# A decoder step with 32 experts on one core: one more weight slot, other turns, and other orders ahead of the experts

## Chip, cores and metric

One core of a Trainium2 chip runs the whole kernel. The metric is the device time of one execution in microseconds, median over runs; lower is better.

## What is computed

One layer of a hybrid decoder over 288 tokens: a prompt of 256 and 8 sequences of 4 new tokens each, all in float32, model width 1024. The reference, cut to what matters:

```python
z = rmsnorm(x, norm_mix_g) @ w_in                    # 1024 -> 2048: q | k | v | u, 512 each
attn = dilated_attention(q, k, v, cache_k, cache_v)  # 8 heads of 64; windows (128,1) (512,4) (2048,16)
ssm  = s5_ssm(u, h0, ...)                            # 32 groups x 64 complex states, diagonal recurrence
g    = gelu(ssm); ssm_o = g * sigmoid(g @ w_glu + b_glu)
x    = x + concat(rmsnorm(attn), rmsnorm(ssm_o)) @ w_out
h    = rmsnorm(x, norm_ffn_g)
gates = softmax(top_4(h @ w_router + b_router))      # 4 of 32 experts
x    = x + sum_over_chosen(gate * (swiglu(h @ w1[e] + b1[e]) @ w2[e] + b2[e]))
y    = rmsnorm(x, norm_final_g)                      # outputs also: k, v and the last states
```

The recurrence has the coefficient a = exp(lambda dt), whose angle is tabulated for 128 steps, and b_bar = ((a - 1)/lambda) b. The experts' weights, 32 x 12 MiB, are most of the memory that is read.

## The kernel before

The program is written engine by engine, with semaphores between them; the order of each engine's work is the order of its code. Its stages, in time:

**Start (0 to 24 us).** SP issues the loads of x (L361: rows 0 to 255 in one transfer; L362: the 32 sample rows), constants, and eleven small parameter loads on one semaphore `prm` (L366 to L383), then w_in in four parts. ACT squares the three row tiles of x with a sum (L616) and takes the square root (L619). DVE makes the reciprocal (L827) and scales the rows, `xn` = x times the scale of its row, in three operations (L829). PE transposes `xn` for eight values of j, three tiles each (`features`, L1275), ACT and DVE bring the result out of PSUM (L623, L841). Between them PE transposes the parameters (`par`, L1283), and after j = 7 the matrix c and the state h0 (L1289).

**Projections and recurrence (24 to 120 us).** PE makes sixteen blocks of the projection (`project(n)`, L1305: 8 products of 128x128 by 288 columns, two instructions each), with the transposition of b_bar after the third (L1314). DVE makes what depends on the parameters (L867 to L903: ar, ai, fr, fi, reciprocal, four products of 256 elements, `xb`), and the last three doublings, levels 4 to 6, of the angle table (`angle_level`, L904 to L911); POOL had made levels 0 to 3 (L526 to L544). Then comes, for eight pairs of groups, a loop over DVE (L928 to L961), POOL (L556 to L595), ACT and PE (`bu`, L1327; `c_h`, L1350).

**Keys and values (101 to 200 us).** Each of the eight cached sequences has five key tiles. `key_columns(n)` (L1385) transposes one tile into PSUM bank 4 + n % 2, ACT or DVE copies it out (`key_tile`, L679), and `scores(b)` (L1402) uses the five of sequence b. The order is by hand: `keys(b)` = tiles 5b to 5b+4, then `scores(b)`. The cached keys of sequence b come in by five DMAs, once the tiles of b - 2 have been transposed (L413 to L416: two buffers, a wait on `kt_ps` in SP's queue).

**Mixer output (188 to 230 us).** DVE gathers the sample rows (L1072), ACT squares the whole of the attention output `aT` (L749), DVE multiplies it by its norm weight (L1076), sums the squares (L1077) and makes two more rows of the gated unit (`glu_rows`); PE then sums over partitions (L1565) and makes the output projection (L1573).

**Router (230 to 257 us), then experts (257 to 1214 us).** Each expert has 12 pieces of 1 MiB of weights. `slots` is a list of NSLOT places of 1 MiB in SBUF, taken from buffers that earlier stages have left; piece k of turn t lies in slot (12 t + k) % NSLOT. SP fills the slots once (`fill`, L445 to L469), each after the wait that says its buffer is free, and then refills a slot when PE has used it (`refill`, L474 to L482, the DMA at L481). An expert has as many passes as its tokens need, by 32 columns a pass, counted at run time: 51 passes for 32 experts, three for experts 0, 4, 8 and others. Only the last pass of an expert lets its slots go. One pass (`pe_pass`, L1703 to L1748) multiplies by w1 (`first_product`, L1708), adds the pass before into the result, gathers the next tokens (L1653) and, after the activation, multiplies by w2 (`second_product`, L1716). The loop over experts is a hardware loop whose body holds TURNS experts one after the other, written out:

```python
with nc.Fori(0, NEXP // TURNS, ...) as g:
    for turn in range(TURNS):
        expert(turn, g * TURNS + turn, g * (16 * TURNS * NPIECE // NSLOT))
```

TURNS x 12 must be a multiple of NSLOT: the slot of a piece is fixed in the code of the body. With NSLOT 20, TURNS is 5: six rounds of five and two experts behind. **Final norm and store (1214 to 1230 us)** end it.

Of the kernel before, what the change touches and what calls it, by code (L numbers as in the profile page):

```python
# [26 lines left out]
ALU = mybir.AluOpType  # L27
# [31 lines left out]
NSLOT = 20  # L59
TURNS = 5  # L60
# [60 lines left out]
def decoder_step(nc, I, O):  # L121

    with ExitStack() as ctx:
# [43 lines left out]
        xn = uni[:, 0:3 * D].rearrange("p (t d) -> p t d", t=3)  # L167
        e_tab = uni[:, 4608:8704].rearrange("p (r i t) -> p r i t", r=2, i=NI)
# [44 lines left out]
        slots = [flat.rearrange("p (m n) -> p m n", m=2) for flat in slots] + [late_slot]  # L213
# [10 lines left out]
        def s5_buf(n):  # L224
# [51 lines left out]
        names = """x con prm win0 win1 wglu wout late gff kload0 kload1 vload0 vload1 vload2 vload3 out ss ms  # L276
# [4 lines left out]
            gex ysv b2 etab_p etab_v gmx con_rest sc osel o_ev yfin  # L281
# [4 lines left out]
        NPRM = 11  # L286
# [73 lines left out]
        def _(sp):  # L360
            sp.dma_start(x[:, 0:2, :], I["x_prompt"][0].rearrange("(t p) d -> p t d", p=P)).then_inc(S["x"], 16)  # L361
# [10 lines left out]
            with nc.allow_non_contiguous_dma(reason="parameters of a few hundred words"):  # L372
                sp.dma_start(gmx, I["norm_mix_g"][0].rearrange("(p j) -> p j", j=J)).then_inc(S["gmx"], 16)
                small(ld[0:NI, 0:2], I["ssm_log_dt"][0].rearrange("(i g) -> i g", g=2))
                small(par[0:NI, 0:P], I["ssm_a_re"][0].rearrange("(i g) n -> i (g n)", g=2))
                small(par[0:NI, P:2 * P], I["ssm_a_im"][0].rearrange("(i g) n -> i (g n)", g=2))
# [7 lines left out]
                sp.dma_start(w_in[:, 3, :, :], wv[:, 3]).then_inc(S["win0"], 16)  # L384
# [82 lines left out]
            fill(18)  # L467
            sp.wait_ge(S["cntr"], 1)
            fill(19)  # L469
# [43 lines left out]
        def _(pool):  # L513
# [10 lines left out]
            pool.memset(top[:, :, :], 0.0)  # L524
            pool.memset(tidx[:, :, :], 0).then_inc(S["zero"], 1)
            pool.wait_ge(S["exps"], 1)  # L526
            link(pool.tensor_copy(e_tab[:, 0, :, 0:1], prm[:, PA_C, :].unsqueeze(2)))
            link(pool.tensor_copy(e_tab[:, 1, :, 0:1], prm[:, PA_S, :].unsqueeze(2)))
            for level in range(4):
                m = 1 << level  # L530
                re, im = e_tab[:, 0, :, 0:m], e_tab[:, 1, :, 0:m]
                cr = bc(e_tab[:, 0, :, m - 1:m], [P, NI, m])
                ci = bc(e_tab[:, 1, :, m - 1:m], [P, NI, m])
                t1, t2 = e_tmp[:, 0, :, 0:m], e_tmp[:, 1, :, 0:m]
                link(tt(t1, re, cr, ALU.mult))
                link(tt(t2, im, ci, ALU.mult))
                link(tt(e_tab[:, 0, :, m:2 * m], t1, t2, ALU.subtract))
                link(tt(t1, re, ci, ALU.mult))
                link(tt(t2, im, cr, ALU.mult))
                ins = tt(e_tab[:, 1, :, m:2 * m], t1, t2, ALU.add)  # L540
                if level == 3:
                    ins.then_inc(S["etab_p"], 1)
                else:
                    link(ins)  # L544
# [64 lines left out]
        def _(act):  # L609
            chain = [0]  # L610

            A = act.activation
            act.wait_ge(S["x"], 32)
            act.wait_ge(S["init"], 1)
            for t, (_, n) in enumerate(TILES):
                ins = A(xn[0:n, t, :], x[0:n, t, :], ACT.Square, accum_out=st[0:n, t:t + 1])  # L616
            ins.then_inc(S["ss"], 1)
# [7 lines left out]
            act.wait_ge(S["prm"], 16 * NPRM)  # L625
# [24 lines left out]

            for n, c in enumerate([12, 13, 14, 15] + list(range(12))):
                if n == 3:
                    act.wait_ge(S["bT_ps"], 1)
                    A(bT[:, :, :], ps[:, 0:2, :], ACT.Copy).then_inc(S["bT"], 1)
# [54 lines left out]
            for n in range(20):  # L709
                key_tile(n)  # L710
# [553 lines left out]
        def _(pe):  # L1264
# [13 lines left out]
            for j in range(4):  # L1278
                features(j)
# [512 lines left out]
```

## Time and profile before

| | us |
|---|---|
| median of 3 runs | 1234.92 (1228.98 to 1236.42) |
| the profiled execution, its own time | 1231.9 |
| its span, first to last instruction | 1230.1 |
| PE busy in the span | 1071.0 (87%) |
| DVE, ACT, POOL busy | 411.3, 219.3, 79.3 |
| HBM read | 442.46 MB |

The span is what the views below divide; 1.8 us lie around it. Times in rows are microseconds from the start of the span. "x64" is a number of instructions (a float32 product is two), and "[1.05 <-DVE uni L1009]" says that the engine had been idle for so long and what released it. PEclk 1.00 is the full granted clock of TensorE.

### The profile page before, as it was taken

The page shows a single profiled execution, that of the slowest core. Times are in us where ns is not written, and L with a number is a line of the kernel's source. Part 1 is how long each engine was busy: PE and PEld are TensorE (multiplying, and loading weights), DVE is VectorE, ACT ScalarE, POOL GpSimd, SP SyncE. Part 2 cuts the span into 40 slices and gives each one's busy share as a digit, 9 for nine tenths or more (in the row PEclk, how much of TensorE's full clock was granted, in tenths as well). Part 3 has the DMA queues.
Part 4 walks back from the last instruction along what each step waited for, and adds up shares of the span by engine and source line. Part 5 has one row for each costly group of instructions (what it writes and reads, how often), then busy time and mean ns, then how long its engine had stood idle before and what let it go on. Part 6 is the DMA issues. An engine that isn't in the chain of part 4 may idle for free.

```text
span 1230.1 us, 29852 instructions
## 1 busy us (share of the span) xinstructions
PE 1071.0 (87%) x10851; PEld 488.5 (40%) x10852; DVE 411.3 (33%) x1236; ACT 219.3 (18%) x401; POOL 79.3 (6%) x117
## 2 busy tenths in 40 slices
PE   5997889999979799989998876899889868998986
PEld 3775454444424244334433321334333323333332
DVE  4899764452222122222222211222222212222212
ACT  3213432311111111111111100011111101111102
POOL 3159500000000000000000000000000000000000
PEclk9999999999999899999999988899999988999978
DMA  8426785855999999999999999999999999999995
GB/s 238 179 86 215 256 304 217 309 207 214 419 420 421 421 384 421 421 421 395 422 420 423 421 421 420 422 385 420 422 422 393 421 421 422 390 421 421 421 419 212
DMA packets 81061, 445.49 MB, mean 362 GB/s; under 512 B 16768, under 2 KB 18112, under 8 KB 32256
## 3 DMA queue, kind: packets, MB, share of 16 engines
q1 hardware_dynamic: 81024, 445.00, 89.7%
q8 instruction: 22, 0.36, 0.1%
q14 instruction: 15, 0.12, 0.0%
HBM read 442.46 MB, written 2.51 MB: 362 GB/s over the span
## 4 chain that ended last, share of the span: by engine, by line
PE 55%; DMA 19%; SPq 16%; issue 4%; DVE 3%; ACT 2%; POOL 0%; DVEq 0%; POOLq 0%; ACTq 0%
PE ps L1708 19%; SPq L481 14%; PE ps L1716 9%; DMA ring<-in_w_moe_dram 8%; DMA low<-in_w_moe_dram 5%; DMA w_glu<-in_w_moe_dram 5%; PE ps L1653 4%; PE ps L1305 4%; PE ps L1701 3%; PE ps L1685 3%; PE ps L1573 2%; DMA ring<-in_cache_k_dram 1%; PE ps L1696 1%; PE ps L1683 1%; PE ps L1733 1%
## 5 line engine op out<-in xcount | busy, mean ns | idle before, releaser
L1708 PE MATMUL ps<-ring,uni 128*32 128x512 f32 x2032 | 249.8, 625 | 63.0 <-issue 32.4
L1708 PEld LDWEIGHTS ps<-ring,uni 128*32 128x32 f32 x2032 | 62.5, 112 | 240.6 <-issue 176.3
L1213 DVE TENSOR_SCALAR uni<-ps 128x256 f32<-128x256 f32 x51 | 21.7, 425 | 312.3 <-PE ps L1708 312.3
L1716 PE MATMUL ps<-ring,uni 128*32 128x256 f32 x1792 | 106.4, 381 | 10.5 <-DMA ring<-in_w_moe_dram 10.4
L788 ACT ACTIVATE uni<-uni 128x256 f32<-128x256 f32 x51 | 21.2, 416 | 417.8 <-DVE uni L1213 417.8
L1234 DVE COPY uni<-ps 128x256 f32<-128x256 f32 x50 | 21.2, 425 | 221.0 <-PE ps L1696 221.0
L788 ACT ACT_TABLE_LOAD x51 | 65.4, 1283 | 85.7 <-issue 85.7
L1653 PE MATMUL ps<-uni 128*32 128x256 f32 x1248 | 78.2, 383 | 0.3 <-DVE uni L1155 0.3
L1716 PEld LDWEIGHTS ps<-ring,uni 128*32 128x32 f32 x1792 | 54.3, 110 | 51.9 <-DMA ring<-in_w_moe_dram 15.3
L1305 PE MATMUL ps<-accT,ring 128*128 128x288 f32 x256 | 64.6, 411 | 0.0
L1685 PE MATMUL ps<-uni 32*128 32x256 f32 x832 | 62.3, 415 | 0.0
L1685 PEld LDWEIGHTS ps<-uni 32*128 32x128 f32 x832 | 39.1, 192 | 48.3 <-issue 46.8
L1701 PE MATMUL ps<-uni 32*32 32x512 f32 x416 | 55.4, 602 | 0.0
L1305 PEld LDWEIGHTS ps<-accT,ring 128*128 128x128 f32 x256 | 48.5, 192 | 14.5 <-issue 1.7
L1228 DVE TENSOR_TENSOR uni<-low,uni 128x96 f32 x50 | 12.9, 259 | 121.0 <-issue 112.7
L792 ACT ACTIVATE uni<-ps 128x256 f32<-128x256 f32 x51 | 19.6, 385 | 183.2 <-PE ps L1716 183.2
L790 ACT ACTIVATE uni<-ps 128x384 f32<-128x384 f32 x51 | 25.0, 491 | 145.1 <-PE ps L1738 145.1
L1653 PEld LDWEIGHTS ps<-uni 128*32 128x32 f32 x1248 | 35.4, 109 | 36.0 <-issue 17.9
L1197 DVE TENSOR_TENSOR uni<-uni 128x64 f32<-128x64 f32 x204 | 44.5, 218 | 1.4
L1222 DVE COPY uni<-ps 128x256 f32<-128x256 f32 x51 | 21.7, 425 | 65.6 <-PE ps L1733 65.6
L1708 PE MATMUL ps<-tmp,uni 128*32 128x512 f32 x320 | 39.8, 613 | 1.1 <-DMA tmp<-in_w_moe_dram 1.1
L1198 DVE TENSOR_TENSOR uni<-uni 32x32 f32<-32x32 f32 x204 | 37.0, 182 | 2.1
(383 smaller groups left out, 1231.9 us busy)
## 6 DMA issues: line engine op xcount, KB each, us to landing
ring<-in_w_moe_dram SPq DMA_DIRECT2D x232, 1024.0 KB, 24.1
tmp<-in_w_moe_dram SPq DMA_DIRECT2D x38, 1024.0 KB, 25.5
kv_rows<-in_w_moe_dram SPq DMA_DIRECT2D x19, 1024.0 KB, 23.2
w_glu<-in_w_moe_dram SPq DMA_DIRECT2D x19, 1024.0 KB, 26.5
mixer<-in_w_moe_dram SPq DMA_DIRECT2D x19, 1024.0 KB, 23.8
uni<-in_w_moe_dram SPq DMA_DIRECT2D x19, 1024.0 KB, 25.7
accT<-in_w_moe_dram SPq DMA_DIRECT2D x19, 1024.0 KB, 26.2
low<-in_w_moe_dram SPq DMA_DIRECT2D x19, 1024.0 KB, 26.6
```

Of the source, the lines that this page charges most:

```text
L481: sp.dma_start(slot(turn, k), piece(following[later - 1], k2)).then_inc(landed(turn, k), 16)
L788: A(sig, glu_b, ACT.Sigmoid, scale=ALPHA).then_inc(S["sgm"], 1)
L790: A(selT, ps[:, 5, 0:3 * P], ACT.Copy).then_inc(S["selT"], 1)
L1197: tt(selg[:, 0:2, q, :], sel[:, 0:2, :], gb[:, 0:2, :], ALU.mult)
L1198: ins = tt(selg[rows, 2, q, :], sel[rows, 2, :], gb[rows, 2, :], ALU.mult)
L1305: ins = mm(ps[:, 4 + n % 2, 0:NTOK], w_in[:, c // 4, j, P * (c % 4):P * (c % 4) + P], accT[:, j, :], start=(j == 0), stop=(j == J - 1))
L1573: ins = mm(ps[:, 4 * t + 2 * a + c, :], src[:, kb, t0:t0 + P], w_out[:, 4 * a + kb, 512 * c:512 * c + 512], start=(kb == 0), stop=(kb == 3))
L1653: ins = mm(ps[quarter(q), 6, 0:NQ], sel[:, t, :], h[:, t, NQ * q:NQ * q + NQ], start=(t == 0), stop=(t == 2), skip_group_check=True)
L1685: ins = mm(ps[:, q, NQ * t:NQ * t + NQ], selT[quarter(q), P * t:P * t + P], y[quarter(q), :], start=False, stop=True, skip_group_check=True)
L1701: mm(hidden(q), pick[quarter(q), :], b1_rows[quarter(q), :].rearrange("p (g n) -> p g n", g=2), start=True, stop=False, skip_group_check=True)
L1708: ins = mm(hidden(q), xe[:, k % 2, quarter(k // 2)], slot(turn, k)[:, :, NQ * q:NQ * q + NQ], start=False, stop=(k == 7), skip_group_check ...
L1716: ins = mm(ps[quarter(q), 7, 0:NQ], mt[:, m, quarter(k - 8)], slot(turn, k)[:, m, NQ * q:NQ * q + NQ], start=(k == 8 and m == 0), stop=(k ...
```

## The change

What it does, in parts:

1. **Ring.** 21 slots in place of 20: the first two tiles of x, 1 MiB, become slot 19, filled after `posps`; the former last slot is slot 20. TURNS is 7: four rounds of seven experts and four behind (84 = 4 x 21).
2. **Start.** x comes in three transfers; the three loads behind dt and lambda have a semaphore of their own (`par`), and the fourth part of w_in is issued right after them. ACT evaluates one square root ahead of everything, squares tile 0 and the sample rows; DVE squares tile 1 by a product and a reduction.
3. **Diagonal.** Rows are no longer scaled: DVE makes three diagonal matrices `scales` (the identity times the scale of each row, at most 128x128), and `features` is a matrix product x by `scales`, which scales and transposes at once.
4. **Order on PE.** features 0 and 1, parameters, features 2 to 7, project(0), transpositions of c and h0, project(1), project(2). ACT, not DVE, brings c and h0 out of PSUM, between its copies of projections 0 and 1.
5. **Parameters and table.** The parameter chain and `xb` go to POOL, but for the reciprocal (DVE, by a handshake `pa`). All levels 0 to 6 of the angle table are on DVE, two copies and seven levels.
6. **Key tiles.** One tile more than a sequence needs is transposed ahead of each `scores`.
7. **Mixer output.** The prompt's part of `aT` is squared and scaled early, only the 32 sample columns behind the last gather; two rows of the gated unit move ahead of the wait or of the sum.

```diff
-NSLOT = 20
-TURNS = 5
+NSLOT = 21
+TURNS = 7
+        scales = uni[:, 3 * D:3 * D + 3 * P].rearrange("p (t c) -> p t c", t=3)
-        slots = [flat.rearrange(...) for flat in slots] + [late_slot]
+        slots = [flat.rearrange(...) for flat in slots] + [x[:, 0:2, :], late_slot]
...
@ SP
-            sp.dma_start(x[:, 0:2, :], I["x_prompt"][0]...).then_inc(S["x"], 16)
+            sp.dma_start(x[:, 0, :], rows[:, 0]).then_inc(S["x0"], 16)
+            sp.dma_start(x[:, 1, :], rows[:, 1]).then_inc(S["x"], 16)
...
             fill(18)
+            sp.wait_ge(S["posps"], 1)
+            fill(19)
             sp.wait_ge(S["cntr"], 1)
-            fill(19)
+            fill(20)
...
@ POOL (in place of levels 0 to 3)
+            pool.wait_ge(S["red"], 1)
+            tt(q(16), q(PA_LR), q(PA_LR), ALU.mult)
+            link(tt(q(17), q(PA_LI), q(PA_LI), ALU.mult))
+            tt(q(16), q(16), q(17), ALU.add).then_inc(S["pa"], 1)
+            pool.wait_ge(S["exps"], 1)
...
+            pool.wait_ge(S["pa"], 2)
+            tt(q(PA_FR), q(18), q(22), ALU.mult)
+            link(tt(q(PA_FI), q(20), q(22), ALU.mult))
+            pool.wait_ge(S["prm"], 16 * NPRM)
+            tt(s3(0), v3(0), fr, ALU.mult)
...
+            ins.then_inc(S["xb"], 1)
...
@ ACT
+            A(st[:, 93:94], st[:, 94:95], ACT.Sqrt)
+            act.wait_ge(S["x0"], 16)
+            A(xn[:, 0, :], x[:, 0, :], ACT.Square, accum_out=st[:, 0:1])
             act.wait_ge(S["x"], 32)
-            for t, (_, n) in enumerate(TILES):
-                ins = A(xn[0:n, t, :], x[0:n, t, :], ACT.Square, accum_out=st[0:n, t:t + 1])
+            A(xn[0:NS, 2, :], x[0:NS, 2, :], ACT.Square, accum_out=st[0:NS, 2:3]).then_inc(S["ss"], 1)
...
             for n in range(20):
                 key_tile(n)
+            key_tile(20)
             prompt_exp(0)
-            key_tile(20)
...
+            act.wait_ge(S["aT"], 4)
+            A(sqa[:, :, 0:SEQ], aT[:, :, 0:SEQ], ACT.Square).then_inc(S["sqA"], 1)
...
@ DVE
+            dve.wait_ge(S["x"], 32)
+            link(tt(xn[:, 1, :], x[:, 1, :], x[:, 1, :], ALU.mult))
+            link(dve.tensor_reduce(st[:, 1:2], xn[:, 1, :], AX, ALU.add))
...
-                ins = ts(xn[0:n, t, :], x[0:n, t, :], st[0:n, 6 + t:7 + t], None, ALU.mult)
+                ins = ts(scales[0:n, t, 0:n], ident[0:n, 0:n], st[0:n, 6 + t:7 + t], None, ALU.mult)
...
-            link(angle_level(4))
-            link(angle_level(5))
+            dve.wait_ge(S["exps"], 1)
+            dve.tensor_copy(e_tab[:, 0, :, 0:1], prm[:, PA_C, :].unsqueeze(2))
+            link(dve.tensor_copy(e_tab[:, 1, :, 0:1], prm[:, PA_S, :].unsqueeze(2)))
+            for level in range(6):
+                link(angle_level(level))
             angle_level(6).then_inc(S["etab_v"], 1)
...
+            scaled(slice(0, SEQ))
...
+            glu_rows(2)
+            dve.wait_ge(S["sqA"], 2)
             dve.wait_ge(S["aTs"], 4)
-            tt(aT[:, :, :], aT[:, :, :], bc(gat.unsqueeze(2), [P, 4, NTOK]), ALU.mult).then_inc(S["mixa"], 1)
+            scaled(slice(SEQ, NTOK)).then_inc(S["mixa"], 1)
+            glu_rows(3)
             dve.tensor_reduce(sums[:, 0, :], sqa.rearrange("p b t -> p t b"), AX, ALU.add)
-            glu_rows(2)
-            glu_rows(3)
...
@ PE
-                    ins = tp(ps[:, 4 + j % 4, t0:t0 + n], xn[0:n, t, j::J], ident[0:n, 0:n])
+                    ins = mm(ps[:, 4 + j % 4, t0:t0 + n], x[0:n, t, j::J], scales[0:n, t, 0:n], start=True, stop=True)
...
+            project(0)
+            natural_transposes()
+            project(1)
+            project(2)
+            pe.wait_ge(S["xb"], 1)
...
-            keys(0)
+            keys(0, 6)
             scores(0)
...
-            keys(1)
+            keys(6, 11)
             scores(1)
-            keys(2)
+            keys(11, 16)
             scores(2)
...
-            keys(3)
+            keys(16, 21)
             scores(3)
...
-            keys(4)
+            keys(21, 25)
...
+            key_columns(25)
             scores(4)
```

In the loop of the last four sequences the tile 5b moves in the same way ahead of `scores(b - 1)`.

## Rows read from the trace of the kernel before

**Rows 1.** Page, part 4: shares of the chain that ended last.

```profile
PE 55%; DMA 19%; SPq 16%; issue 4%; DVE 3%; ACT 2%; POOL 0%; DVEq 0%; POOLq 0%; ACTq 0%
```

**Rows 2.** Windows: stretch, PE, PEld, DVE, ACT, POOL busy, clock, DMA share, GB/s.

```profile
255.00:290.00 35.00, 33.39 (x390) 14.01 (x394) 13.09 (x56) 6.43 (x9) 0.00 (x0) 1.00 0.18 71
...
440.00:446.00 6.00, 6.00 (x60) 1.79 (x54) 1.88 (x10) 1.67 (x2) 0.00 (x0) 1.00 0.62 221
...
561.00:568.00 7.00, 7.00 (x74) 2.25 (x70) 2.05 (x10) 1.67 (x2) 0.00 (x0) 1.00 0.78 307
...
803.00:809.00 6.00, 6.00 (x62) 1.84 (x58) 1.79 (x9) 1.67 (x2) 0.00 (x0) 1.00 0.61 227
...
926.00:931.00 5.00, 5.00 (x48) 1.46 (x48) 1.50 (x9) 0.90 (x1) 0.00 (x0) 1.00 0.75 242
...
1047.00:1053.00 6.00, 6.00 (x54) 1.78 (x58) 2.05 (x10) 1.66 (x2) 0.00 (x0) 1.00 0.70 255
1053.00:1210.00 157.00, 141.00 (x1532) 60.22 (x1524) 35.74 (x136) 20.60 (x32) 0.00 (x0) 0.93 1.01 421
```

**Rows 3.** Timeline of SP, 398 to 450 us: start, length, instruction, count.

```profile
415.79 0.39 SPq L481 DMA_DIRECT2D low<-in_w_moe_dram  x1
443.07 5.47 SPq L481 DMA_DIRECT2D ring<-in_w_moe_dram  x7
```

**Rows 4.** Chain of waits in the expert stage: start, length, piece.

```profile
273.38 7.01 PE ps L1708 x64
...
289.11 7.00 PE ps L1708 x64
```

**Rows 5.** Chain of waits, 440 to 600 us.

```profile
457.59 1.32 issue
```

**Rows 6.** Timeline, 1186 to 1231 us: the last product.

```profile
1213.67 3.66 PE L1716 MATMUL ps<-ring,uni 128*32 128x256 f32 x64
```

**Rows 7.** Timeline, 5 to 24 us: squares, table load, row scaling.

```profile
6.95 1.06 ACT L616 ACTIVATE uni<-x 128x1024 f32<-128x1024 f32 x1 [3.42 <-DMA x<-in_x_sample_dram]
...
10.20 1.28 ACT L619 ACT_TABLE_LOAD   x1
...
11.94 2.06 DVE L829 TENSOR_SCALAR uni<-x,st 128x1024 f32<-128x1024 f32 x3
```

**Rows 8.** Timeline of PE from 13 us: transpositions, first products of project(0).

```profile
14.15 3.51 PE L1275 MATMUL ps<-low,uni 128*128 128x128 f32 x12 [14.15 <-DVE uni L829]
...
23.64 1.17 PE L1305 MATMUL ps<-accT,ring 128*128 128x288 f32 x2
```

**Rows 9.** Timeline, 0 to 60 us: projections 0 to 2; angle table; pair 0.

```profile
23.64 12.38 PE L1305 MATMUL ps<-accT,ring 128*128 128x288 f32 x48
...
44.30 1.22 DVE L911 TENSOR_TENSOR uni<-tmp 128x1024 f32<-128x1024 f32 x1
...
48.15 0.69 DVE L941 TENSOR_TENSOR ring<-ring 128x512 f32<-128x512 f32 x1
```

**Rows 10.** Timeline, 60 to 125 us: pair 2 waits; the same operations beside POOL.

```profile
67.30 1.29 DVE L936 TENSOR_TENSOR ring<-ps,uni 128x512 f32<-128x512 f32 x2 [1.16 <-PE ps L1327]
...
79.82 1.19 DVE L941 TENSOR_TENSOR ring<-ring 128x512 f32<-128x512 f32 x1
...
93.44 1.38 POOL L558 TENSOR_TENSOR tmp<-ring,low 128x128 f32<-128x128 f32 x1
```

**Rows 11.** Timeline of PE, 100 to 262 us: transpositions of key tile 35.

```profile
171.94 1.09 PE L1385 MATMUL ps<-low,ring 128*128 128x128 f32 x8 [0.94 <-DMA ring<-in_cache_k_dram]
```

**Rows 12.** Waits of PE, 100 to 200 us: total, times, longest.

```profile
PE ps L1402 <- ACT ring L679: 3.5, 5, 0.8
```

**Rows 13.** Timeline of PE: sums of squares, then the output projection.

```profile
202.28 0.62 PE L1565 MATMUL ps<-ring,mixer 128*32 128x512 f32 x2 [1.69 <-issue]
...
205.25 0.62 PE L1565 MATMUL ps<-ring,mixer 128*32 128x512 f32 x2 [1.05 <-DVE uni L1009]
207.16 7.13 PE L1573 MATMUL ps<-ring,mixer 128*128 128x512 f32 x16
```

More of the change, by code:

```diff
@@ L524, in _ @@
             pool.memset(top[:, :, :], 0.0)
+            pool.memset(cT[:, :, :], 0.0)
             pool.memset(tidx[:, :, :], 0).then_inc(S["zero"], 1)
-            pool.wait_ge(S["exps"], 1)
[L527 to L544, printed above, removed]
+            q = lambda n: prm[:, n, :]
@@ new lines, in _ @@
+            s3 = lambda n: ssm_hi[:, 0, 256 * n:256 * n + 256].rearrange("p (i c) -> p i c", i=NI)
+            s4 = lambda n: ssm_hi[:, 1, 256 * n:256 * n + 256].rearrange("p (i c) -> p i c", i=NI)
+            tt(s3(0), v3(0), fr, ALU.mult)
+            tt(s3(1), v3(1), fi, ALU.mult)
+            tt(s4(0), v3(1), fr, ALU.mult)
+            link(tt(s4(1), v3(0), fi, ALU.mult))
+            for g in range(2):
+                rows = slice(64 * g, 64 * g + 64)
+                dst = lambda r: xb[rows, r, :].rearrange("p (i g c) -> p i g c", i=NI, g=2)[:, :, g, :]
+                tt(dst(0), s3(0)[rows], s3(1)[rows], ALU.subtract)
+                ins = tt(dst(1), s4(0)[rows], s4(1)[rows], ALU.add)
@@ L649, in decays, with natural_out @@
                 ins.then_inc(S["dec"], 1)
+            def natural_out():
+                act.wait_ge(S["prmT"], 2)
+                act.wait_ge(S["zero"], 1)
+                A(h0[:, :, :], ps[:, 1, 0:2 * P].rearrange("p (r n) -> p r n", r=2), ACT.Copy).then_inc(S["bT"], 1)
+                for r in range(2):
+                    for g in range(2):
+                        rows = slice(64 * g, 64 * g + 64)
+                        apart = lambda flat: flat.rearrange("p (k g c) -> p k g c", g=2, c=16)[:, :, g, :]
+                        A(apart(cT[rows, r, :]), apart(ps[rows, 2 + r, :]), ACT.Copy, scale=1.0 - 2.0 * r)
             for n, c in enumerate([12, 13, 14, 15] + list(range(12))):
+                if n == 1:
+                    natural_out()
                 if n == 3:
@@ L748, in _ @@
             act.wait_ge(S["aTs"], 4)
-            A(sqa, aT[:, :, :], ACT.Square).then_inc(S["sqA"], 1)
+            A(sqa[:, :, SEQ:], aT[:, :, SEQ:], ACT.Square).then_inc(S["sqA"], 1)
             gate(3)
@@ L1064, in _, with scaled @@
             pair_out(3)
+            def scaled(cols):
+                n = cols.stop - cols.start
+                return tt(aT[:, :, cols], aT[:, :, cols], bc(gat.unsqueeze(2), [P, 4, n]), ALU.mult)
+            dve.wait_ge(S["sqA"], 1)
+            dve.wait_ge(S["aT"], 4)
+            scaled(slice(0, SEQ))
             dve.wait_ge(S["osel"], 1)
@@ L1307, in project @@
                 ins.then_inc(S["proj"], 1)
-            for n in range(3):
-                project(n)
-            pe.wait_ge(S["xn"], 4)
+            project(0)
[3 more added lines that the diff above has]
+            pe.wait_ge(S["xb"], 1)
+            pe.wait_ge(S["bT"], 1)
             for r in range(2):
@@ L1386, in key_columns, with keys @@
                 ins.then_inc(S["kt_ps"], 1)
-            def keys(b):
-                for n in range(5 * b, 5 * b + 5):
+            def keys(first, end):
+                for n in range(first, end):
                     key_columns(n)
```

103 lines of the change are left out of this document (39 added, 64 removed).

## The prediction

> **What bounds the kernel now.** I read the chain of waits first. PE has 55% of it, DMA 19% and SP's queue 16% [rows 1]: two limits, in different stages, so no share of the whole says what the change is worth. The windows show which is where. Up to 255 the work is a hand-ordered chain around PE. From 290 on the weights come at 421 GB/s, up to 1210, with five dips [rows 2]. At 421 GB/s, 1 MiB takes 1.0486 MB / 421.5 = 2.49 us. PE alone would be much shorter: a pass takes 289.11 - 273.38 = 15.73 us [rows 4], entering a new expert 1.32 more [rows 5], so 51 passes and 32 entries are 802.2 + 42.2 = 844 us, while the stage lasts from 257.6 (one pass ahead of 273.38) to 1217.3 [rows 6]. The stream is the bound there, and the end moves with the stream's idle time and with its start, nothing else.
>
> Where is it idle? In each dip, the lost time is the window times (1 - rate/421.5): 6 x (1 - 221/421.5) = 2.85, then 7 us at 307: 1.90, 6 at 227: 2.77, 5 at 242: 2.13, 6 at 255: 2.37; together 12.0 [rows 2]. SP's timeline tells why: it issues one refill at 415.79 and the next only at 443.07, 27.3 us later, then seven in a row [rows 3]. It waited for PE to let a slot go, through an expert with three passes, which keeps its pieces until the last one; the queue's backlog ran out before that. And before 290 the ring is full and the DMA almost still, 71 GB/s in 35 us [rows 2], for the same reason (expert 0 has three passes).
>
> **Ring.** One more slot holds one more MiB in flight whenever SP would stop. At the start that is 2.49 us of the stream done before the first refill. In each dip it takes away up to 2.49 us of idle: 2.49 + 1.90 + 2.49 + 2.13 + 2.37 = 11.4. Sum -13.9. Between dips PE waits for the stream, so the ring is empty when the next three-pass expert comes and each dip counts anew. Bounds: -2.5 (the first MiB alone) and -14.5 (all dips closed, 12.0 + 2.49). I take -13.9. The added slot 19 waits for `posps` in SP's queue, behind it is only the fill that already waits for a later event, so nothing is held up. Writing out 7 experts in place of 5 costs nothing if an entry stays 1.32; PE has 959.7 - 844 = 116 us of room, 3.6 us per entry.
>
> **Start.** Before: squares from 6.95 (3.23 us for three), a table load of 1.28 at 10.20, row scaling 11.94 to 14.00, features from 14.15 [rows 7, 8]. After: one transfer more is issued ahead of the last x (an issue is 0.39, [rows 3]), so x is there at about 7.4; DVE multiplies 1024 elements, 1.22 by the table's operation of that size [rows 9], and reduces them, same size, 1.3; ready at 10.0, with ACT's share beside it. No table load is left. Root, reciprocal and small operations took 11.94 - 11.48 = 0.5 plus 0.2 ahead; three scalings of 128 instead of 1024 elements, 2.06 before, about 0.75. Features begin at 11.5: -2.65.
>
> **Features as products.** A transposition of one j (three tiles) took 3.51 / 4 = 0.88 us [rows 8]. A float32 product is two instructions where a transposition is one, so one j is 1.75 at that rate. That rate is the slow one: 12 instructions in 3.51 us, against 8 full ones in 1.09 later [rows 11]; the first two products of project(0) took 0.585 each, all 48 together 12.38, 0.258 on average [rows 8, 9]. So the level rose from 1.2 to 2.4 GHz, by these durations, inside project(0), with products and not with transpositions ahead. If the features' products raise it too, I take 2.3 of the 8 js at 1.75 and 5.7 at 0.8: 8.6, plus 0.4 for the parameters: project(0) at 20.5 instead of 23.64. Then three projections at (12.38 - 1.17)/46 = 0.244 an instruction, 11.7, and the moved transpositions of c and h0 at the fast rate, 1.1 where they took twice that: `xb`'s transpositions at 33.3, before 23.64 + 12.38 = 36.0. I take -2.5, start included. If the clock stays low through the features, 14.0 + 0.4 from 11.5 gives project(0) at 25.9, and 26.0 + 0.6 + 11.7 + 1.1 = 39.5: +3.5. Bounds -2.8 and +3.5. In SP's queue the fourth part of w_in is now issued ahead of eight parameter loads; b, c and h0 are used after 24, so I price that at nothing, and bound it, with the other parts of w_in that project(4) asks for 2.5 us sooner, by +2.5: then the start gains nothing.
>
> On this the Trainium skill has a rule: "TensorE: Matmul & The Clock Gate", Part 4, says that a transposition does not count as PE work for the clock gate. The trace agrees (0.29 us an instruction to the end of them, fast only after products began); by it the features as products count, and the low end of the two sums is the likelier.
>
> **Parameters and table.** On DVE the doublings have six operations each. From 1.22 for 1024 elements and 0.69 for 512 (another operation, same form) [rows 9] the fixed part is 0.16: levels 6 to 0 take 6 x (1.22 + 0.69 + 0.43 + 0.29 + 0.23 + 0.19 + 0.18) = 19.4 us. They start when the exponentials are there, about 20: done near 39.5, where the last operation ended at 45.52 before [rows 9]. PE comes to `bu(0)` at 33.3 + 0.9 + 3.9 + 1.1 = 39: no wait of size, PE stays the bound of the first pairs, as the 1.16 us that DVE waits for it in pair 2 shows [rows 10]. POOL's chain is some 12 small operations and 8 of 256 columns. A POOL operation of 128x128 cost 1.38 beside a busy DVE [rows 10]; bounds for `xb`: at 28 if POOL is twice as fast alone, at 35 if all eight cost 1.4 and the rest 0.3. PE asks at 33.3. I take 31, no wait; at 35 it is +1.7.
>
> The row on sharing: the same DVE operation took 0.69 with POOL still and 1.19 with it busy [rows 9, 10]. "SBUF — State Buffer", section "SBUF: two separate sides", of the Trainium skill says that DVE with two SBUF inputs and GpSimd take one port pair in turn, whole instructions at a time. It speaks against this part, and the trace agrees. By it, 10 POOL operations would hold the table up by about 5 us, to 45, where it was before: the price is then still nothing, but the gain above is gone.
>
> **Key tiles.** `scores(b)` waits for the copy of its last tile, five times, 3.5 us in all [rows 12]; with one tile more between, that goes: -3.5. Against it, tile 5b now comes one `scores` sooner and its cached keys do not: at tile 35 PE waited 0.94 for that DMA already [rows 11]. What was hidden behind the score, about 1.0 (near the 1.09 of eight transpositions), and its wait of 0.7 come back as DMA wait, in about three sequences: 3 x 1.7 = 5.1. Sum +1.6; bounds -3.5 and +6.
>
> **Mixer output.** PE waits 1.69 for the scaled `aT` and 1.05 for the sums, and begins the projection at 207.16 [rows 13]. Now the operations behind the gather have 32 of 288 columns, and two rows of the gated unit fill the waits: 1.69 + 1.05 and some 0.75 of the DVE work between, -3.5; bounds -1.05 and -4.
>
> **Sum.** Front -2.5 + 1.6 - 3.5 = -4.4 (ends -10.3 and +8.5, which don't come together). It moves the first pass, and so the whole stream. With the ring, -18.3: 1231.9 - 18.3 = 1213.6 for an execution like the profiled one, which is 3.0 under the median of the runs: 1216.6.
>
> **Rivals.** (1) The ring gives only the first MiB: the dips stay because another thing than the slot ends them, for instance PE runs later in each by what the stream gained. For: a slot more also lets the stream run ahead to the same stop. Against: SP's 27 us without an issue [rows 3] are a wait for a slot. 1231.9 - 2.5 - 4.4 + 3.0 = 1228.0. (2) Clock low in the features and key tiles late: +3.5 + 4 - 3.5 = +4 ahead of the experts; 1231.9 - 13.9 + 4 + 3.0 = 1225.0. For: the 0.94 of [rows 11]; against: the rise inside project(0) [rows 8, 9]. (3) Slower: the loop's body grows by two experts of written-out code, and an entry, 1.32 us of "issue" without any named releaser [rows 5], grows with it. PE becomes the bound: 253.2 + 802.2 + 32e + 14.6 behind the last product (1231.9 - 1217.3). It decides from e = 4.5, reaches the time before at 5.1; at 5.5 the sum is 1246.0, 1249 by the median. For: the pause has no other cause in the view; against: it is the same length anywhere in the body.
>
> **How the numbers follow.** Forecast 0.62, rival 1 0.17, rival 2 0.13, rival 3 0.08. Low end: best bounds, 1231.9 - 14.5 - 10.3 + 3.0 = 1210, less 4 because the runs of before scatter 6 us below their median: 1206. High end 1232: both rivals of the same sign and half of their scatter. Within 1% of 1234.92 (1222.6 to 1247.3, about what a measurement can tell from no change): most of rivals 1 and 2, and little of the forecast, 0.24; faster 0.70; slower 0.06.
>
> **What would show it.** Right: dips in the windows' GB/s that are 2.5 us of traffic shallower, 421 from 286 on; SP's longest pause near 25; features from 11.5 and project(0) at 20.5; key scores without ACT waits but DMA waits at tiles 10, 30 and 35; the output projection near 203. Wrong: five dips of the same area (rival 1), features of 1.75 to the end (2), entries of 4 us and PE near 100% busy after 290 (3).

## The result, and the profile after

The changed kernel takes 1241.31 us (median of 5 runs, 1239.11 to 1245.9) against 1232.81 us before (5 runs, 1228.98 to 1236.42): 1.0062 times as long, 95% interval 1.0036 to 1.0088. Forecast were 1216.6 us. The span of the profiled execution is 1237.8 us, 7.7 longer than before.

First the page of the kernel after: the shares of the chain (part 4), and ahead of them two lines of part 3, which I had not read for the prediction: the queues that fetch instructions, with packets, MB and their share of 16 engines.

```profile
q8 instruction: 65, 1.06, 0.4%
q14 instruction: 48, 0.39, 0.1%
...
PE 59%; DMA 15%; SPq 13%; issue 7%; DVE 3%; ACT 1%; DVEq 1%; POOL 0%; POOLq 0%
```

And these two lines of the page of the kernel before:

```profile
q8 instruction: 22, 0.36, 0.1%
q14 instruction: 15, 0.12, 0.0%
```

The chain has nearly the shares of [rows 1]; "issue" has risen from 4 to 7%. The instruction packets have tripled: 22 to 65 on q8, 15 to 48 on q14. In the trace's DMA packets q8, which serves PE (e6 below), moves 16,384 bytes at a time and q14, which serves DVE (e10, e14) and perhaps others, 8,192. The last packet of the kernel before ahead of the loop's end is at 369 us, the next at 1161: the loop of five experts ran 792 us without one. In the kernel after they come all through the loop.

The windows of the kernel after that answer to [rows 2] (stretch, busy PE, PEld, DVE, ACT, POOL, clock, DMA share, GB/s):

```profile
262.00:297.00 35.00, 34.07 (x397) 14.40 (x401) 11.54 (x49) 6.37 (x9) 0.00 (x0) 1.00 0.22 82
447.00:450.00 3.00, 3.00 (x32) 0.91 (x28) 0.26 (x1) 0.00 (x0) 0.00 (x0) 1.00 0.97 366
567.00:576.00 9.00, 9.00 (x110) 3.41 (x106) 2.04 (x10) 1.67 (x2) 0.00 (x0) 1.00 0.42 155
813.00:819.00 6.00, 6.00 (x58) 1.93 (x58) 2.04 (x10) 1.67 (x2) 0.00 (x0) 1.00 0.68 242
936.00:945.00 9.00, 9.00 (x110) 3.27 (x103) 2.04 (x10) 1.67 (x2) 0.00 (x0) 1.00 0.54 192
1062.00:1065.00 3.00, 3.00 (x33) 0.91 (x28) 0.26 (x1) 0.00 (x0) 0.00 (x0) 1.00 0.90 325
1065.00:1220.00 155.00, 142.79 (x1607) 63.38 (x1599) 37.85 (x143) 21.48 (x34) 0.00 (x0) 0.97 1.01 420
```

By the same sum, the dips lose 0.4 + 5.7 + 2.6 + 4.9 + 0.7 = 14.3 us, where they lost 12.0. The first and the last are nearly closed, as forecast for all; two have grown to 9 us of width, 80 and 30 us behind the starts of rounds of seven experts (487 and 906 us, counted in PE's passes). Between the dips the stream is a little slower as well. One window of before and the one that answers to it after:

```profile
446.00:561.00 115.00, 106.20 (x1240) 45.28 (x1235) 29.57 (x110) 16.36 (x26) 0.00 (x0) 0.99 1.01 422
```

```profile
450.00:567.00 117.00, 104.32 (x1193) 45.11 (x1189) 29.30 (x109) 16.34 (x26) 0.00 (x0) 0.97 1.01 419
```

From the first dip to the end it is 419 or 420 GB/s after, and 421 or 422 before; over some 740 us that is, as an estimate, 3 us. With 2.3 more in the dips and 2.5 less for the first MiB of the new slot that makes 2.8 more, and the stage has 2.4 more (974.9 against 972.5, below). The stage starts later too, and a pass has its old length, as in [rows 4]. The chain of the kernel after, first the second and third pass, then the start of the second round:

```profile
278.72 7.00 PE ps L1727 x64
...
294.45 7.00 PE ps L1727 x64
```

```profile
461.95 5.55 issue
...
469.68 2.72 issue
...
473.19 2.21 PE ps L1672 x24
...
482.47 4.86 issue
487.33 8.77 PE ps L1727 x64
```

And SP's timeline in the same place, refills (start, length of the queue's work, count):

```profile
466.69 9.03 SPq L486 DMA_DIRECT2D ring<-in_w_moe_dram  x4
...
480.38 4.99 SPq L486 DMA_DIRECT2D x<-in_w_moe_dram  x1
```

One refill took 0.39 in [rows 3]; here one takes 4.99. DVE stands still for 5.55 and 2.72 with nothing to wait for, PE waits for it and then stands still itself for 4.86 as it enters the next expert, where [rows 5] had 1.32.

Ahead of the experts, the timeline of the kernel after, start, for [rows 7 to 9]:

```profile
6.61 1.23 DVE L861 TENSOR_TENSOR uni<-x 128x1024 f32<-128x1024 f32 x1 [4.44 <-DMA x<-in_x_sample_dram]
...
9.78 0.62 DVE L869 TENSOR_SCALAR uni<-low,st 128x128 f32<-128x128 f32 x3
...
10.54 3.77 PE L1286 MATMUL ps<-uni,x 128*128 128x128 f32 x12 [10.54 <-DVE uni L869]
...
14.64 11.23 PE L1286 MATMUL ps<-uni,x 128*128 128x128 f32 x36
```

```profile
43.72 1.22 DVE L914 TENSOR_TENSOR uni<-tmp 128x1024 f32<-128x1024 f32 x1
...
62.52 1.29 DVE L940 TENSOR_TENSOR ring<-ps,uni 128x512 f32<-128x512 f32 x2 [5.81 <-PE ps L1344]
```

The products of `features` are first issued at 10.54 (before: 14.15), yet they last to 25.9; project(0) begins at 26.5 (before: 23.64), and the transpositions of `xb` at 41.1 (before: 35.9). The angle table is done at 44.9 (before: 45.5), and DVE waits 5.8 us for PE's `bu` in pair 1.

The waits of PE between 105 and 212 us, for [rows 11, 12], and the output projection, for [rows 13]:

```profile
PE ps L1402 <- DMA ring<-in_cache_k_dram: 5.1, 2, 3.1
...
PE ps L1419 <- ACT ring L713: 0.2, 1, 0.2
```

```profile
212.49 7.13 PE L1592 MATMUL ps<-ring,mixer 128*128 128x512 f32 x16
```

### The profile page after: what moved, and what is told of

Read it like the earlier page. It is cut to its first block, busy times and chain, and to the rows that moved or that the text cites. A ratio compares the mean times of both kernels' runs of the same rounds, so it can differ in the third digit from the quotient of the medians.

```text
span 1237.8 us, 29884 instructions
## 1 busy us (share of the span) xinstructions
PE 1083.5 (88%) x10875; PEld 502.3 (41%) x10876; DVE 411.0 (33%) x1240; ACT 219.5 (18%) x405; POOL 79.9 (6%) x114
## 4 chain that ended last, share of the span: by engine, by line
PE 59%; DMA 15%; SPq 13%; issue 7%; DVE 3%; ACT 1%; DVEq 1%; POOL 0%; POOLq 0%
PE ps L1727 19%; SPq L486 12%; PE ps L1735 10%; DMA ring<-in_w_moe_dram 9%; PE ps L1672 4%; PE ps L1319 4%; PE ps L1704 3%; PE ps L1720 3%; DMA uni<-in_w_moe_dram 2%; DMA low<-in_w_moe_dram 2%; PE ps L1592 2%; PE ps L1715 1%; PE ps L1702 1%; PE ps L1752 1%; PE ps L1286 1%
## 5 line engine op out<-in xcount | busy, mean ns | idle before, releaser
L1727 PE MATMUL ps<-ring,uni 128*32 128x512 f32 x2008 | 246.7, 628 | 56.4 <-issue 39.7
L1735 PE MATMUL ps<-ring,uni 128*32 128x256 f32 x1696 | 100.5, 381 | 9.1 <-DMA ring<-in_w_moe_dram 9.0
L1672 PE MATMUL ps<-uni 128*32 128x256 f32 x1248 | 81.2, 394 | 9.3 <-DVE uni L1239 9.0
L1735 PEld LDWEIGHTS ps<-ring,uni 128*32 128x32 f32 x1696 | 51.7, 110 | 48.8 <-DMA ring<-in_w_moe_dram 14.3
L1727 PE MATMUL ps<-tmp,uni 128*32 128x512 f32 x320 | 41.1, 628 | 10.4 <-issue 6.2
## 6 DMA issues: line engine op xcount, KB each, us to landing
uni<-in_w_moe_dram SPq DMA_DIRECT2D x18, 1024.0 KB, 25.9
x<-in_w_moe_dram SPq DMA_DIRECT2D x18, 1024.0 KB, 26.5
```

Of the source, the lines that this page charges most:

```text
L1672: ins = mm(ps[quarter(q), 6, 0:NQ], sel[:, t, :], h[:, t, NQ * q:NQ * q + NQ], start=(t == 0), stop=(t == 2), skip_group_check=True)
L1727: ins = mm(hidden(q), xe[:, k % 2, quarter(k // 2)], slot(turn, k)[:, :, NQ * q:NQ * q + NQ], start=False, stop=(k == 7), skip_group_check ...
L1735: ins = mm(ps[quarter(q), 7, 0:NQ], mt[:, m, quarter(k - 8)], slot(turn, k)[:, m, NQ * q:NQ * q + NQ], start=(k == 8 and m == 0), stop=(k ...
```

## The experiments

Expert stage means, here and below, the time from the first product of the first expert to the end of the span. It is 972.5 us before (1230.1 - 257.59) and 974.9 after (1237.8 - 262.93). The kernel before was run again beside each group of experiments, with medians of 1233.4 to 1234.5 us; the ratios below are against those runs.

| kernel | slots, turns | median us | stage us | q8, q14 packets |
|---|---|---|---|---|
| before | 20, 5 | 1232.8 | 972.5 | 22, 15 |
| after | 21, 7 | 1241.3 | 974.9 | 65, 48 |
| e1 ring alone | 21, 7 | 1235.2 | 973.5 | 62, 48 |
| e2 new front alone | 20, 5 | 1264.1 | 996.9 | 68, 41 |
| e3 | 20, 10 | 1247.6 | 984.5 | 63, 49 |
| e4 | 18, 3 | 1261.2 | 999.9 | 19, 14 |
| e5 | 18, 9 | 1277.8 | 1013.9 | 64, 47 |
| e6 waits on PE | 20, 5 | 1240.1 | 980.5 | 68, 15 |
| e7 waits on DVE, ACT, SP | 20, 5 | 1259.7 | 994.8 | 22, 40 |
| e8 front, transposed | 20, 5 | 1256.7 | 997.1 | 22, 40 |
| e9 the same, padded | 20, 5 | 1238.9 | 972.2 | 22, 18 |
| e10 output part | 20, 5 | 1254.1 | 992.5 | 22, 40 |
| e11 products ahead | 20, 5 | 1236.4 | 976.0 | 22, 15 |
| e12 key order | 20, 5 | 1236.3 | 972.2 | 22, 15 |
| e13 output part, padded | 20, 5 | 1236.2 | 972.2 | 22, 17 |
| e14 the same, DVE alone | 20, 5 | 1237.2 | 973.0 | 22, 16 |
| e15 output part, DVE in three places | 20, 5 | 1230.9 | 971.7 | 22, 16 |

The stage is that of one profiled execution each. With 20 slots and a loop that is not fetched again it lies between 971.7 and 973.0, but at 976.0 in e11, so a difference of 3 or 4 us in this column says little by itself.

**e1, the ring alone.** The kernel before with

```diff
-NSLOT = 20
-TURNS = 5
+NSLOT = 21
+TURNS = 7
```

and slot 19 and the two fills of the change.

> The kernel before with the ring of 21 slots and 7 written-out turns, nothing else. Theory A (the longer loop body has to be fetched again by DMA each round, and the engines stand still meanwhile): the expert stage is not shorter than before, within 973 to 976 us from the first product to the end instead of 972.5, new dips near the ends of the rounds of seven experts, whole time 1233 to 1237. Theory B (the ring works as I had worked it out, and the loss is all ahead of the experts): the stage is 14 us shorter, whole time near 1219.

Ratio 1.0008 (0.9991 to 1.0024): the ring alone gives nothing, and the packets have tripled. Theory A holds.

**e2, the new front alone.** The kernel after with NSLOT 20 and TURNS 5.

> The kernel after with the ring of 20 slots and 5 turns of the kernel before: only the other orders ahead of the experts. Theory A (features as products at the low clock and key tiles cost 5.3 us together): first product of the experts at 262.9, expert stage 972.5, whole time 1238 to 1240. Theory B (the front is not the cause and its later start is taken up by the stream): whole time near 1233.

Neither theory: 1.0251 (1.0209 to 1.0294). The first product comes at 265.8, but the stage, whose code is that of the kernel before, is 24.4 us longer, and both instruction queues fetch all through it. The loop has not become longer. What differs is what stands ahead of it: 48 instructions more on PE (24 products, each two loads and two multiplications, in place of 24 transpositions of one and one), 5 more on DVE and, by my count, on ACT (the trace records 4 more there), 1 on SP. This gives a new theory, C: where the loop begins within the fetched packets decides whether it stays.

**e3, the code alone.** The kernel before with

```diff
-TURNS = 5
+TURNS = 10
```

> The kernel before, 20 slots, with 10 turns written out in place of 5: the same ring, twice the code in the loop. Theory A (code fetches): more packets in the instruction queues than the 22 and 15 of before, waits of several us in PE, DVE and SP around the ends of rounds, 5 to 20 us slower. Theory B (code length costs nothing): within 2 us of the kernel before.

1.0115 (1.009 to 1.014), stage +12.0 at the same ring: twice the code in the loop costs 12 us.

**e4 and e5, 18 slots with 3 and with 9 turns.** NSLOT 18, the two last fills left out.

> The kernel before with 18 slots and 3 turns: a shorter body and two slots less. By the working for the ring, two slots less cost 2 x 2.49 at the start and up to 2 x 2.49 in each of five dips, in all about 25 to 30 us plus new dips where the ring held so far: near 1260. Theory A adds that the stalls of some us at expert entries that the kernel before still has (1.3 us each) get rarer or stay; if short code gives back much, it is near 1250 or less.

> The kernel before with 18 slots and 9 turns, against the run with 18 slots and 3 turns (1261.2 us; expert stage 999.9 us; no instruction fetch from 325 to 1206 us). Same ring, three times the code in the loop. Theory A (the loop's code does not stay on the chip and is fetched again in each round): over 100 instruction packets in place of 33, and the stage 10 to 25 us longer. Theory B (the number of turns is free): same time within 2 us.

At equal rings, 9 turns cost 14.0 us of stage more than 3. And e4 has the size of the ring without any fetch: 999.9 - 972.5 = 27.4 us for two slots, 13.7 for one. That is the term I had worked out as 13.9. If one slot more is worth as much as one slot less costs, which no run shows by itself, then e1 says that its 7 turns cost 973.5 - 972.5 + 13.7 = 14.7, near the 12.0 and 14.0 of e3 and e5.

**e6, 48 met waits on PE.** The kernel before with

```diff
-            pe.wait_ge(S["con"], 16)
+            for _ in range(97):
+                pe.wait_ge(S["con"], 16)
```

(two waits stand in one instruction: 96 waits more are 48 instructions more by the page's count, 29900 against 29852).

> The kernel before with 48 instructions more on PE at its very start, each a wait on a semaphore that is already met, in time in which PE is idle; the loop of the experts then begins 48 instructions later, as in the kernel with the new front alone. Theory C (where the loop stands in memory decides how much of it is fetched again): PE's instruction queue fetches all through the expert stage, about 65 packets in place of 22, and the stage is longer by 5 to 20 us. Theory D (the 24 us of the run with the new front alone come from something else in it): 22 packets, time as before, within 2 us.

1.0054 (1.0032 to 1.0077), stage +8.0, q8 68 packets, q14 15 as before. So theory C holds for PE.

**e7, waits on DVE, ACT and SP.** The kernel before with ten more `dve.wait_ge(S["con"], 16)` and ten more `act.wait_ge(S["init"], 1)` ahead of their first waits, and one `sp.wait_ge(S["proj"], 8)`.

> The kernel before with 5 instructions more at the start of DVE, 5 of ACT and 1 of SP, all waits already met: these engines' loops begin where they begin in the kernel with the new front alone. Theory C: the second instruction queue fetches in each round of five experts, with DVE standing still 5 us a packet, and the expert stage is longer by 5 to 20 us, the rest of the 24. Theory D: 15 packets as before, same time.

1.0199 (1.0163 to 1.0235): eleven instructions that do nothing make the kernel 25.7 us slower, 22.3 of them in the stage. Not all else was left as it was ahead of it: ACT's first table load, at 2.25 before, now stands behind the wait for x, and the first transposition starts at 15.58 in place of 14.15. That is 1.4 of the 3.4 us that remain.

```profile
7.08 1.28 ACT L618 ACT_TABLE_LOAD   x1 [6.95 <-DMA x<-in_x_sample_dram]
```

The page of e7:

```profile
q8 instruction: 22, 0.36, 0.1%
q14 instruction: 40, 0.33, 0.1%
```

DVE's timeline at the start of its second round, and the largest waits of PE from 300 to 1200 us:

```profile
390.35 0.19 DVE L1202 TENSOR_TENSOR uni<-uni 32x32 f32<-32x32 f32 x1
402.93 0.26 DVE L1232 TENSOR_TENSOR uni<-low,uni 128x96 f32 x1 [12.39 <-issue]
```

```profile
PE ps L1712 <- issue: 44.9, 28, 2.7
PE ps L1712 <- DMA ring<-in_w_moe_dram: 30.2, 29, 1.5
PE ps L1657 <- DVE uni L1232: 14.7, 4, 5.4
```

DVE stands still for 12.4 us; the trace has q14 packets at 393.6, 395.6, 400.6 and 405.7, the last three 5 us apart, while the weights' queue is full. Each packet moves in 0.33 us but comes only every 5 us. It looks as if the engine has to have one before it asks for the next; no run tests that. PE waits for DVE in four places, 14.7 us together, a wait that the kernel before does not have.

**e8, the diagonal undone** (on e2):

```diff
-ts(scales[0:n, t, 0:n], ident[0:n, 0:n], st[...], None, ALU.mult)
+ts(xn[0:n, t, :], x[0:n, t, :], st[...], None, ALU.mult)
-mm(ps[...], x[0:n, t, j::J], scales[0:n, t, 0:n], start=True, stop=True)
+tp(ps[...], xn[0:n, t, j::J], ident[0:n, 0:n])
```

> The new front with 20 slots and 5 turns (1264.1 us), with the diagonal undone: DVE scales the rows, three operations of 1024 elements, and PE transposes them. Theory (a product costs two instructions where a transposition costs one, both at the low clock): features from 12.0 instead of 10.5, end 6.5 - 1.5 = 5 us earlier, first product of the experts near 261. Theory C adds that PE's loop then stands where it stood before, so that its fetches end near 365 and the stage is 5 to 20 us shorter than the 996.9 of the new front alone. Rival: the clock rises no earlier, project(0) starts only 2 us sooner, and the stage stays at 997.

1.0178 (1.0149 to 1.0207), 7.4 us under e2. PE's timeline:

```profile
11.99 1.77 PE L1284 MATMUL ps<-low,uni 128*128 128x128 f32 x6 [11.99 <-DVE uni L867]
...
14.10 5.27 PE L1284 MATMUL ps<-low,uni 128*128 128x128 f32 x18
20.01 5.85 PE L1317 MATMUL ps<-accT,ring 128*128 128x288 f32 x16 [0.64 <-ACT accT L642]
...
44.46 13.35 PE L1317 MATMUL ps<-accT,ring 128*128 128x288 f32 x48 [1.43 <-DMA ring<-in_w_in_dram]
```

project(0) starts at 20.0 in place of 26.4. But project(4), at 44.46, waits 1.43 for w_in and starts where it did before, at 44.3. Of the start's gain nothing is left. q8 is back at 22 packets and q14 still at 40, and the stage is 997.1 against 996.9, as the rival in the expectation had it. So beside the fetches of q14 those of PE cost nothing here, though alone they cost 8.0 (e6): the two don't add.

**e9, e8 padded** by 123 instructions on DVE and ACT and 127 on SP, waits already met, in idle time.

> The new front with transposed features (1256.7 us, expert stage 997.1 us) with 123 instructions more on DVE and ACT, and 127 on SP, all waits already met, in stretches in which these engines are idle: with the 5, 5 and 1 that the new front has more than the kernel before, each loop is moved by 128 instructions of 64 bytes, one fetched packet of 8192 bytes. Theory C (the position of the loop within the packets decides): the fetches of the second instruction queue stop near 370 us as in the kernel before, the expert stage is near 973, whole time 1233 to 1238. Rival (more code ahead of the loop is what costs): stage still near 997, whole time 1257 or more.

1.004 (1.002 to 1.006): 17.8 us faster than e8, with 373 instructions more that do nothing. The page:

```profile
q8 instruction: 22, 0.36, 0.1%
q14 instruction: 18, 0.15, 0.0%
```

The stage is 972.2. This decides for theory C: more code ahead of the loop is not what costs; moved by 128 instructions against the kernel before, the loop stands where it stays. The time is a little over the 1233 to 1238 expected; what the padding itself costs is seen in e13. 128 fill one packet of 8,192 bytes if each has 64 bytes; the Trainium skill ("Runtime: NRT & Kernel Launch", "Instruction fetch mechanics") counts 256 to 16 KiB, which is the same size of an instruction.

**e10, the output part alone** (the change's lines between `rows_of(1)` and the sums, on the kernel before).

> The kernel before with the change's mixer output alone: 2 instructions more on DVE ahead of the loop, 1 on ACT. Output projection 2.7 us sooner against the keys. If the kernel before has a margin of at least two instructions, 1231 us; if not (theory C with the edge at once), instruction packets of the second queue all through the experts and 1250 to 1258 us.

1.0163 (1.013 to 1.0196). The output projection came 3.9 us sooner after the first key tile (206.5 - 114.7, against 207.16 - 111.4), and the stage was 20.0 us longer. The edit has two instructions more on DVE and one on ACT; e14 shows that it was DVE's two.

**e11, products ahead.** Seven products of `ones` by `ones` into bank 7 before PE's first wait.

> The kernel before with seven products of 128x128 by 512 columns of ones on PE from 2 us on, into an unused bank, in the time in which PE waits for x; nothing else is changed. If PE's low clock at the start comes from its idle time ahead, the transpositions from 14.2 us take 272 ns (as in the key tiles) instead of 421 and end near 20 instead of 23.4; if it does not depend on what PE did, 421 as before. The 28 instructions more move PE's loop: fetches all through the experts as in the run with 48 waits, 6 us more at the end.

1236.41 us (one run). PE's timeline:

```profile
2.22 9.34 PE L1269 MATMUL ps<-ones 128*128 128x512 f32 x14 [2.22 <-DVE st L821]
13.61 2.85 PE L1278 MATMUL ps<-low,uni 128*128 128x128 f32 x12 [2.05 <-DVE uni L829]
...
16.79 3.54 PE L1278 MATMUL ps<-low,uni 128*128 128x128 f32 x12
```

The first twelve transpositions take 0.24 us each instead of 0.29 in [rows 8], the second twelve 0.295 again. The windows of e11 show the granted clock itself, 1.00 and then 0.50 (busy times as in [rows 2], clock third from the end):

```profile
8.00:15.00 7.00, 4.95 (x15) 2.28 (x14) 3.33 (x8) 4.61 (x8) 0.00 (x0) 1.00 0.90 191
...
18.00:25.00 7.00, 7.00 (x25) 5.16 (x24) 3.75 (x12) 1.87 (x5) 4.59 (x18) 0.50 0.76 189
```

So the level can be raised ahead. It fell between 15 and 16 us, after 2.05 us of idle time and about 2 us of transpositions, and which of the two did it e11 doesn't tell. The fetches that I expected did not come (22 packets): 28 instructions are not too many for PE; 48 are.

**e12, the key order alone** (PE's calls and `key_tile(20)` of the change; as many instructions as before).

> The kernel before with the change's order of key tiles alone, number of instructions on each engine as before. My step: +1.6 us (the waits for the copies of the last tile go, 3.5, and DMA waits come at tiles 10 and 35, 5.1). Rival: the waits for cached keys only shift, time the same within 1 us. No effect on the instruction queues in either case, 22 and 15 packets.

1.0022 (1.0003 to 1.004), +2.9 us. PE's waits, 110 to 212 us:

```profile
PE ps L1385 <- DMA ring<-in_cache_k_dram: 6.7, 4, 3.6
```

There are 6.7 us of DMA waits in 4 places, and the 3.5 us of waits for ACT's copies are no longer among the larger waits, as in the step of my prediction.

**e13, e14, e15, the output part with its loop kept.** e13: 126 waits on DVE in one place and 127 on ACT; e14: those on DVE alone; e15: 126 on DVE in three places (15, 36, 75).

> The kernel before with the change's mixer output, and 126 instructions more on DVE and 127 on ACT (waits already met, in idle time ahead of the router), so that with the 2 and 1 of the edit each loop is moved by 128. Theory C: instruction packets 22 and about 17, expert stage 972.2 as in the two runs that keep their loops, output projection 3.9 us sooner against the key tiles: 1230 us, 3 to 4 under the kernel before. Rival: what is gained ahead of the experts is taken by the landing of the first weights, time as before.

> The same with the 126 instructions on DVE alone; ACT's loop stands one instruction later than in the kernel before. If DVE's loop alone did the damage in the run of the output part (1254.1 us), this one is like the run padded on both, 1230 us; if ACT's loop is at its edge too, fetches of the second queue come in each round, with ACT standing still, and the time is 1235 to 1255.

> The mixer output alone, once more with 126 instructions more on DVE, now in three places (15 while DVE waits for x, 36 ahead of the sums over partitions, 75 ahead of the last rows of the output projection), since in one place they took 12.5 us in a wait of 9 and delayed the router by 3.3 us. Theory: the loops stay, expert stage 972.2, first product of the experts 3 to 4 us sooner against the key tiles: 1230 to 1232 us against 1234 for the kernel before. Rival: the landing of weights sets the start of the stage, and the time is as before.

e13 1.0022 (1.0006 to 1.0037), e14 1.0031 (1.0017 to 1.0046): in both the loop stays (stage 972.2 and 973.0; q14 17 and 16), so DVE's loop alone did the damage of e10, but the padding itself took 12.5 us in a wait that was 9.3 before, and held up the rows ahead of the router:

```profile
236.52 1.28 DVE L1116 SCALAR_TENSOR_TENSOR x<-ps,st,x 128x1024 f32<-128x1024 f32 x1 [12.54 <-issue]
```

e15 has 1230.94 us, ratio 0.9967 (0.995 to 0.9984): faster than the kernel before by 0.3% and than the changed one by 0.8%. e13 is 2.1 us over its kernel before and e15 3.6 under: the place of the padding alone is 5.7 us. The output part is the one part of the change that a run shows to be worth keeping, and it needs 126 empty instructions.

## Why the prediction was wrong

**Ring, -13.9.** The term agrees with what a slot less costs, 13.7 us (e4 against before, by half of two slots), and in the changed kernel the first dip and the last are nearly closed; a cost that the sum had put at nothing took it back. What failed is the sentence "Writing out 7 experts in place of 5 costs nothing if an entry stays 1.32". Rival 3 had the right cause, more written-out code, and the wrong form: I let each of 32 entries grow, by a pause whose cause no row showed. In fact the loop, or part of it, is fetched again in each round; the stalls are about 5 us a packet in DVE, SP and PE around the starts of rounds, and with what follows from them the 7 turns cost 14.7 us (e1, by the slot of e4). The page of the kernel before had the evidence: 22 and 15 packets for a kernel of 1230 us. A kernel whose loop runs with no fetch has something to lose by a longer one.

The Trainium skill has a rule on this that I had left out of the working: "Runtime: NRT & Kernel Launch", section "Instruction fetch mechanics", gives an instruction memory of 32 KiB for most engines and 128 KiB for PE, refilled by 16 KiB, and says that a taken branch to a target outside the two pages held forces a fetch before execution can go on. The runs agree in the stall (e3, e5, e7), and in 16 KiB packets on q8. They differ in one point: q14's packets have 8 KiB. That a loop that fits is kept, the section doesn't say outright; the runs show it (no packet in 792 us), within a placement that two instructions can spoil.

**Start and features, -2.5.** Measured +5.2 at the transpositions of `xb` (41.09 against 35.86). Features began sooner than forecast (10.54; I had 11.5). The step that failed is "If the features' products raise it too": the products stayed at 0.443 us, 0.31 apart, from 10.54 to 25.9, and the count of PE's products in 1 us rose from 3 to 9 only between 29 and 33 us, inside project(0), which took 5.9 us for its 16 instructions (at the full level 0.244 each, 3.9). The bound of +3.5 had the mechanism (rival 2) and was 1.6 too low, since project(0) itself started slow. The level of these products is read from their durations: the clock row reads 1.00 there in spite of them, in both kernels. Their weight loads bear it out, 0.332 us each, where those of project() take 0.190 at the median and 0.337 at most.

The rule on transpositions that the prediction cited ("TensorE: Matmul & The Clock Gate", Part 4, of the Trainium skill) doesn't carry what I took from it. It does not follow from it that these products would raise the level, and here they did not. Nor does every run bear it out: e15, whose start is that of the kernel before but for waits, was fast at its last transposition, ahead of any product:

```profile
22.17 0.42 PE L1305 MATMUL ps<-low,h0row 128*128 128x128 f32 x1
...
23.21 0.27 PE L1305 MATMUL ps<-low,h0row 128*128 128x128 f32 x1
```

What decides when the level rises no run here shows.

Even with the diagonal undone (e8) the start gives nothing, since project(4) waits for w_in: the bound of +2.5 that I had put beside it, and not taken.

**Parameters and table, 0.** Right in the price, since PE stayed the bound, and late in the working: the table was done at 44.9 and not near 39.5. DVE began it at 24.5 and not at 20, because it stood waiting for the slow features (3.05 and 3.20 us) to copy them out. Sharing with POOL showed only while both ran: DVE's operations of 16 columns took 0.55 to 0.72 us beside POOL's of 256, and 0.18 otherwise. POOL's took 0.62; `xb` was ready near 28.8, at the low end of my bounds, and PE did not wait.

**Key tiles, +1.6.** Right in sign and mechanism, +2.9 in e12, with an interval that nearly reaches nothing (from 0.4).

**Mixer output, -3.5.** Right: -3.6 in e15 (interval -6.2 to -2.0), 3.9 by the rows of e10.

**Front, -4.4.** By e1 against the kernel after, same ring and same code length, it is +6.1: 1241.3 - 1235.2. About +5 from the diagonal, +2.9 from the keys, -3.6 from the output make +4 to +5. The diagonal by itself is 7.4 us, e2 against e8 at equal stages. e9, which has the new front without it, fits the same sum: +2.9 - 3.6 and the 5.7 that padding in that place costs make +5.0, and it has +5.4. What is left is within what fronts differ by in profiled executions: the first product came at 257.6 to 263.6 in before, e1, e3, e4, e5 and e11, whose fronts are equal up to e11's products. Part of that is the granted clock, which between 235 and 258 us was 0.93 in before, 0.78 in e1 and 0.80 in e5. In sum the ring's term came out 14 to 15 us short and the front's 10.5: 25, the whole miss of 24.7.

Open: which part of a round is fetched for which engine beyond DVE, why a packet takes 5 us to come, and how far each loop stands from its edge. PE takes 28 instructions more (e11) and not 48; for DVE 2 are too many (e10, e14) and 1 was not tried; ACT takes 1 (e14). A loop that stays with other code ahead of it was shown for a shift of 128 alone. A ring of 21 slots with a loop that stays was not tried: 21 slots need 7 turns.

## What to carry to other kernels

Before a hardware loop is made longer, or anything is put ahead of it, read the instruction queues in the page: a loop that runs without instruction packets has a cliff beside it, here 20 us of the stage for two more instructions on DVE (e10) and 22 for eleven empty ones (e7), since beside a full weight stream a packet that moves in 0.33 us came only every 5. Test the placement by itself, with met waits, before judging an edit by its time; otherwise one edit's time is another's cliff (the output part alone measured +1.6% and is worth -0.3%). And an edit that starts an early stage sooner is worth nothing past the next transfer that was just in time.

## What the runs showed of the hardware that I had not expected

- Five, five and one instructions of met waits on DVE, ACT and SP, executed once near the start, made the expert stage 22.3 us longer (e7, 994.8 against 972.5); 373 such instructions elsewhere made another one 17.8 us faster (e9 against e8).
- Instruction packets of 8,192 bytes take 0.33 us each, but while the weight queue is full the next comes 5.0 us later: 395.6, 400.6, 405.7 in e7.
- 126 wait instructions of DVE took 12.5 us in e13, 0.1 us each.
- 48 instructions of products, with 128x128 or 32x128 weights by 128 or 32 columns, back to back for 15 us, left TensorE at its lower level, by their durations (0.443 us each, weight loads 0.332).
- After 9.3 us of transpositions alone, the last one before the first product took 0.27 us in e15, and 0.42 in the kernel before at the same place.
